# The last steps of the reciprocal root at the norms between blocks: on VectorE, in line with their use, and not on GpSimd

## What is computed

```python
def rmsnorm(x, g):
    xf = x.astype(jnp.float32)
    y = xf * lax.rsqrt(jnp.mean(xf * xf, axis=-1, keepdims=True) + EPS)
    return (y * g.astype(jnp.float32)).astype(x.dtype)

def second_block(x, ...):
    for i in range(DEPTH_2):
        h = rmsnorm(x, norm_mixer_pre[i])
        ...                                  # m = attention or convolution of h
        x = x + rmsnorm(m, norm_mixer_post[i])
        h = rmsnorm(x, norm_mlp_pre[i])
        x = x + rmsnorm(sq_relu_mlp(h, mlp_w_up[i], mlp_w_down[i]), norm_mlp_post[i])
    return x
```

## Time and profile before

| | us |
|---|---|
| Median of 3 runs | 2257.68 (2257.19 to 2259.3) |
| Profiled execution, its own time | 2260.75 |
| Its span, first to last instruction | 2259.0 |

### The profile page before, as it was taken

The page is one execution under the profiler, slowest core; times in us unless marked ns, Lnnn a source line. Parts: engine busy times, 40 slices in busy tenths (PEclk is TensorE's granted clock), DMA queues, the critical chain, the costliest instruction groups (busy, mean ns, idle before and its releaser), DMA issues.

```text
span 2259.0 us, 23194 instructions
## 1 busy us (share of the span) xinstructions
PE 2103.7 (93%) x9629; PEld 1740.1 (77%) x9629; DVE 1047.4 (46%) x930; ACT 751.8 (33%) x923; POOL 153.9 (7%) x311
## 2 busy tenths in 40 slices
PE   6998989989999999899887989999979977999997
PEld 5777778878888888688665778888868866888886
DVE  3345567654443243547544353333352355433434
ACT  3344463343323132422354342322341224322322
POOL 1000132000100000300000120000030003000001
PEclk9999999999999999899765989999989998999999
DMA  5211112123333222233100222332213222222331
GB/s 178 80 56 56 56 56 75 58 93 103 94 97 107 94 93 93 80 109 89 70 0 1 75 75 95 104 100 93 93 56 106 99 82 77 94 93 93 99 105 56
DMA packets 91339, 188.24 MB, mean 83 GB/s; under 512 B 3598, under 2 KB 3616, under 8 KB 91136
## 3 DMA queue, kind: packets, MB, share of 16 engines
q1 hardware_dynamic: 87744, 176.17, 23.6%
q0 software_dynamic: 3232, 10.21, 1.5%
q10 hardware_dynamic: 288, 0.79, 0.1%
HBM read 184.01 MB, written 2.10 MB: 82 GB/s over the span
## 4 chain that ended last, share of the span: by engine, by line
PE 81%; DVE 8%; ACT 4%; issue 3%; POOL 3%; DMA 1%; SPq 0%; POOLq 0%; ACTq 0%; DVEq 0%
PE ps L664 55%; PE ps L788 8%; PE ps L676 5%; PE ps L689 4%; PE ps L983 2%; PE ps L1012 1%; PE ps L892 1%; DVE w_lo L1456 1%; ACT w_hi L1058 1%; POOL small L516 1%; PE ps L714 1%; ACT qk L1123 1%; POOL small L518 1%; PE ps L816 1%; PE ps L843 1%
## 5 line engine op out<-in xcount | busy, mean ns | idle before, releaser
L1456 DVE TENSOR_TENSOR w_lo<-w_raw,w_hi 128x2048 fp32r<-128x2048 f32 x140 | 320.8, 2292 | 834.3 <-ACT w_hi L1058 834.3
L1058 ACT ACTIVATE w_hi<-w_raw 128x2048 fp32r<-128x2048 f32 x140 | 268.2, 1916 | 995.3 <-PE ps L664 877.3
L664 PE MATMUL ps<-a_hi,w_hi 128*128 128x512 f32 x1104 | 429.5, 389 | 0.0
L664 PE MATMUL ps<-a_lo,w_hi 128*128 128x512 f32 x1104 | 429.5, 389 | 0.0
L664 PE MATMUL ps<-a_hi,w_lo 128*128 128x512 f32 x1104 | 429.5, 389 | 0.0
L664 PE MATMUL ps<-w_hi,h_hi 128*128 128x512 f32 x672 | 262.9, 391 | 12.9 <-DVE h_lo L1500 9.3
L664 PE MATMUL ps<-w_lo,h_hi 128*128 128x512 f32 x672 | 262.5, 391 | 0.0
L664 PE MATMUL ps<-w_hi,h_lo 128*128 128x512 f32 x672 | 262.4, 390 | 0.0
L664 PEld LDWEIGHTS ps<-a_hi,w_hi 128*128 128x128 f32 x1104 | 207.2, 188 | 43.2
L664 PEld LDWEIGHTS ps<-a_lo,w_hi 128*128 128x128 f32 x1104 | 207.2, 188 | 42.8
L664 PEld LDWEIGHTS ps<-a_hi,w_lo 128*128 128x128 f32 x1104 | 207.2, 188 | 42.8
(11 more groups left out here) (299 smaller groups left out, 3153.9 us busy)
## 6 DMA issues: line engine op xcount, KB each, us to landing
w_raw<-in_w_ff SPq DMA_DIRECT2D x32, 1024.0 KB, 5.3
w_raw<-in_mlp_w_up SPq DMA_DIRECT2D x32, 1024.0 KB, 5.5
w_raw<-in_mlp_w_down SPq DMA_DIRECT2D x32, 1024.0 KB, 5.0
w_raw<-in_w_in SPq DMA_DIRECT2D x26, 1024.0 KB, 5.0
w_raw<-in_attn_w_qkv SPq DMA_DIRECT2D x12, 1024.0 KB, 5.3
w_raw<-in_conv_w_in SPq DMA_DIRECT2D x12, 1024.0 KB, 5.1
w_raw<-in_w_proj_gla SPq DMA_DIRECT2D x4, 1024.0 KB, 5.1
w_raw<-in_w_out SPq DMA_DIRECT2D x4, 1024.0 KB, 5.0
```

Of the source, the lines that this page charges most:

```text
L664: last = mm(ps[:, bank0 + j], left, right, start=(k == 0 and x == 0), stop=(k == QUAD * quads - 1 and x == 2), skip_group_check=halves)
L1058: nc.scalar.activation(w_hi[:, s], w_raw[:, s], ACT.Copy).then_inc(hi_ready, 1)
L1456: tt(w_lo[:, s], w_raw[:, s], w_hi[:, s].bitcast(F32), ALU.subtract).then_inc(lo_ready, 1)
```

## The change

The five instructions of a refinement leave GpSimd's queue and are issued by DVE, with the same operands, ahead of the instruction that multiplies the tile. DVE no longer waits for `rstd_ready`; it waits for ACT's sum ahead of the first of the five and for ACT's guess ahead of the second. Each of the five is followed by a wait of DVE for its own completion (`step`). GpSimd keeps its transfers. Nothing else is changed.

```diff
         @block.gpsimd
...
-            def refine(name, n, i):
-
-                pool.wait_ge(sumsq_ready, stat_count(name, n, i))
-                v, y, t, r, ss = (z[n % 2][:, i:i + 1] for z in (var, guess0, newton, rstd, sumsq))
-                pstep(nc.gpsimd.tensor_scalar(v, ss, 1.0 / D, EPS, ALU.mult, ALU.add))
-                pool.wait_ge(guess_ready, stat_count(name, n, i))
-                pstep(nc.gpsimd.tensor_tensor(t, y, y, ALU.mult))
-                pstep(nc.gpsimd.tensor_tensor(t, t, v, ALU.mult))
-                pstep(nc.gpsimd.tensor_scalar(t, t, -0.5, 1.5, ALU.mult, ALU.add))
-                nc.gpsimd.tensor_tensor(r, t, y, ALU.mult).then_inc(rstd_ready, 1)
...
             gain_row(g_turn, "norm_mlp", 0)
-            refine_tiles("h_mlp0")
             pool.wait_ge(normed, 8)
...
+            def tile_rstd(name, n, i):
+
+                dve.wait_ge(sumsq_ready, stat_count(name, n, i))
+                v, y, t, r, ss = (z[n % 2][:, i:i + 1] for z in (var, guess0, newton, rstd, sumsq))
+                step(ts(v, ss, 1.0 / D, EPS, ALU.mult, ALU.add))
+                dve.wait_ge(guess_ready, stat_count(name, n, i))
+                step(tt(t, y, y, ALU.mult))
+                step(tt(t, t, v, ALU.mult))
+                step(ts(t, t, -0.5, 1.5, ALU.mult, ALU.add))
+                step(tt(r, t, y, ALU.mult))
+
             def junction(name, move, rows, last_split, early_split=None):
...
                     if add is not None and 1 <= s_ <= TT:
                         i = s_ - 1
-                        dve.wait_ge(rstd_ready, stat_count(name, add, i))
+                        tile_rstd(name, add, i)
                         r = rstd[add % 2][:, i:i + 1]
...
                     if turn_ is not None and 2 <= s_ <= TT + 1:
                         i = s_ - 2
-                        dve.wait_ge(rstd_ready, stat_count(name, turn_, i))
+                        tile_rstd(name, turn_, i)
                         stt(y_tm[:, i], x_tm[:, i], rstd[turn_ % 2][:, i:i + 1], g_turn, ALU.mult, ALU.mult).then_inc(normed, 1)
```

More of the change, by code:

```diff
@@ L505, in _ @@
             dma = pool.dma_start
-            pstep = Steps(pool, pool_step)
             def gain_row(dst, name, row=None):
@@ L542, in _ @@
             assert r == N_GAINS
-            refine_tiles("h")
             pool.wait_ge(turned, turn_base["h"] + 8)
@@ L587, in _ @@
             gain_row(g_turn, "norm_mixer_pre_2", 0)
-            refine_tiles("h_mix1")
             pool.wait_ge(resid_ready, 4)
@@ L603, in _ @@
             gain_row(g_turn, "norm_mlp_pre_2", 0)
-            refine_tiles("h_mlp1")
             pool.wait_ge(normed, 16)
@@ L607, in _ @@
             gain_row(g_turn, "norm_mixer_pre_2", 1)
-            refine_tiles("h_conv")
             pool.wait_ge(chunk_lo, 4 + 2 * 16 + 8)
@@ L611, in _ @@
             gain_row(g_turn, "norm_mlp_pre_2", 1)
-            refine_tiles("h_mlp2")
             pool.wait_ge(normed, 24)
             gain_row(g_add, "norm_mlp_post_2", 1)
-            refine_tiles("out")
         @block.tensor
```

## The result

The changed kernel takes 2267.07 us (median of 8 runs, 2265.47 to 2269.05), the kernel before in the same session 2258.36 (8 runs): a ratio of 1.0037, 95% interval 1.0028 to 1.0045. A second session gave 2265.35 for 2259.38, 1.0026 (1.0015 to 1.0036). One run of the kernel before, in the session of e9 to e11, took 4185.09 us and is left out of the ratios there. The change costs 6 to 9 us. The forecast, 2268.5, lies within 1.5 us of the first median and 3.2 of the second, but as a difference it said 10.8 us, more than either interval holds.

A forecast was written before the change was run, and what follows sets the result against it. PE was taken to bound the kernel, DVE only at seven places; delays of 4.95 + 1.90 + 0.95 + 0.40 + 1.80 = 10.0 us plus 0.8 for the clock, on 2257.68, gave 2268.5 us, range 2264.2 to 2272.7.

The forecast's parts named there:

- What bounds the kernel, and which row decides: PE paces the kernel; DVE's staircase matters at seven places, decided by L1586 of tile 2, in `out` the last L1581.
- The price of a refinement on DVE: Five small DVE instructions 0.19 us apart cost 0.95 us per refinement, 0.76 after the guess where DVE comes early.
- The walk: DVE's staircase followed row by row through the junctions: decisive L1586 of `h_conv` 1.62 us later, `out` 1.80 later.
- The start: Junction `h`: tiles 1 and 2 do not hide their refinements, 1.90 us later, plus 0.8 us for TensorE's clock.
- The 0.8 for the clock: In `h`, longer PE idle time ahead of each tile brings a lower granted clock at restart, costing 0.8 us.
- Later decisive row is later product: In `h_mlp1`, `h_conv`, `h_mlp2` PE's restart follows the later L1586: 3 x 1.65 = 4.95 us.
- by a few tenths of a us, either way: At places other than `h`, where the clock is already down, a later restart shifts its rise only this much.
- The shared port: Rival: the five instructions vanish into gaps left by stretched GpSimd instructions; at a 0.10 step -3.6 us, 2254.1; chance 0.04.
- Absorbed: Rival: PE's restart hangs on something other than L1586 of tile 2; about 2.5 us remain, 2260.2; chance 0.09.
- The clock takes more: Rival: longer PE pauses bring the low clock into `h_mlp0` and `h_mix1` too; 14.5 us, 2272.2; chance 0.08.
- outside the junctions no stretch changed: Sign: the stretches between junctions keep their length, everything else being paced by PE and shifting with it.
- Its other signs: 220 small DVE instructions, 33 us more busy time; PE's transposes wait about 80 us; GpSimd's busy time less than half.

The follow-up runs named there:

- e9: Kernel before with the refinement in three instructions on GpSimd everywhere but in `h_mix1`, which keeps five: 2254.11 us for 2258.91, ratio 0.9974.
- e11: The kernel before itself, unchanged, one profiled execution for a second profile; its stretch from `h_mix1` to `h_mlp1` took 324.62 us.
- e5: Changed kernel with one more small instruction in each of the 44 refinements, six in place of five: 2276.37 us for 2259.14, ratio 1.0076.
- second pair: Second profile of the changed kernel (e12) against the second of before (e11); the shifts kept sum to 8.5 us.
- e12: The changed kernel again, unchanged, for a second profile and more times: 2265.35 us for 2259.38, ratio 1.0026.
- e1: Kernel before with the refinement moved to VectorE only in the first junction, `h`: 2260.27 us for 2258.50, ratio 1.0007.
- e2: Kernel before with the refinement moved to VectorE only in `h_mlp1`, `h_conv` and `h_mlp2`: 2261.79 us for 2258.50, ratio 1.0013.
- first pair: First profile of the changed kernel against the first of before; the shifts kept sum to 7.7 us.
- e10: Kernel before with the refinement in three instructions on GpSimd in `h_mix1` alone: 2260.09 us, ratio 1.0007.
- e6: Changed kernel with the refinement on VectorE in three instructions in place of five: 2263.85 us, ratio 1.0020.

## Why the prediction was right, and where it was not

- **What bounds the kernel, and which row decides.** Right: the loss comes from the places named, each decided by the row named. Nothing outside them took new instructions, but two stretches without one changed their length, see below.
- **The price of a refinement on DVE.** Right: 0.95 us at 0.19 per step. e5's sixth instruction moved the decisive row by 6 x 0.19 = 1.14 us, as the forecast counts six refinements ahead of it in line. The Trainium skill (VectorE: DVE Perf Modes, "The TRN2 errata") gives the duration of an fp32 tensor_tensor as (N + 151) cycles at 0.96 GHz; the estimate from it for one element, 0.158 us, agrees with the means of 0.146 to 0.160 us measured.
- **The walk.** Right: decisive rows 1.69 (1.62), 0.97 (0.95), 0.43 (0.36), 1.82 (1.80) us later.
- **The start.** `h`: the third turn instruction 1.91 us late in the second pair (forecast 1.9), and 2.1 us kept in the mean of the profiles, forecast 1.9 + 0.8. The 0.8 for the clock can be seen at PE's restart. The restart and the row at which the matmuls turn from 0.41 to 0.28 us, before and in the changed kernel:

```profile
24.64 0.56 PE L689 MATMUL ps<-a_hi,w_hi 128*128 128x256 f32 x1
25.22 0.31 PE L689 MATMUL ps<-a_hi,w_lo 128*128 128x256 f32 x1
...
27.07 0.56 PE L662 MATMUL ps<-a_hi,w_hi 128*128 128x256 f32 x1
31.28 0.38 PE L662 MATMUL ps<-a_lo,w_hi 128*128 128x256 f32 x1
```

They stand 0.21 us apart ahead of that row and 0.12 behind it. So the product of the kernel before, too, began at the lower clock, for 0.6 us (1.2 in e11), and not at the full one as the forecast read from the 1.00 of the earlier trace rows; that column shows 1.00 for the changed kernel from 25 to 31 us as well, where the matmuls stand 0.21 apart. The slow part is 4.2 us there, 2.9 in e12 and 2.5 in e1. From the third turn instruction to the first `w_lo` it takes 11.41, 10.78 and 10.61 us in these three, 9.74 and 10.09 in the two profiles of before; the restart itself stands 2.95 us behind that instruction in all five. So the clock took 0.5 to 1.7 us. Behind that, in a stretch that varies by 3.4 us between profiles with the same `h`, part of it is lost from sight.
- **"Later decisive row is later product", for the three junctions.** This term was mis-sized: 4.95 us in the sum, 3.2 kept in e2 and 3.2 in the second pair, 5.1 in the first pair. Likewise 0.40 for `h_mix1`, of which -0.26 to +0.26 was kept, and 0.95 for `h_mlp0`, of which 0.6 to 1.4 was. The step that failed is the sentence that at these places a later restart moves the clock's rise "by a few tenths of a us, either way". It is up to 1.4 us, and it does not average out here: without `h`, the decisive rows are 8.2 to 8.3 us late in both pairs, and 7.7 and 6.6 are kept; in e2 it is 5.1 and 3.2.
- **What makes up the difference.** `h_conv` shows both signs. At its restart the product runs longer at the lower clock, and 2.0 to 2.5 us are kept where 1.69 went in. Behind it, at the start of the last product ahead of `h_mlp2`, 1.1 to 1.4 come back. The kernel before, PE's timeline:

```profile
1842.04 0.77 PE L664 MATMUL ps<-w_hi,h_hi 128*128 128x512 f32 x1 [8.59 <-DVE h_lo L1500]
...
1847.72 0.52 PE L664 MATMUL ps<-w_lo,h_hi 128*128 128x512 f32 x1
```

and the changed one:

```profile
1847.07 0.77 PE L637 MATMUL ps<-w_hi,h_hi 128*128 128x512 f32 x1 [7.18 <-DVE h_lo L1473]
...
1850.62 0.48 PE L637 MATMUL ps<-w_hi,h_lo 128*128 128x512 f32 x1
```

The row of 0.52 and that of 0.48 us are where matmuls turn from 0.63 us (lower clock) to 0.39 (upper). It took 5.68 us from the restart in before and 3.55 us in the changed kernel. Of the 2.1 us in which before still ran slow, 1.0 us is lost time, and that is the 1.06 given back.
- **The rivals.** The shared port: GpSimd's instructions were indeed held by DVE's, and taking them away did win 0.3 us ahead of the first L1565, but the step of 0.19 decides, as worked out. Absorbed: wrong as put, since every decisive row moved. The clock takes more: wrong in the sign of its sum. It was the right mechanism with only one of its two directions, and so was the forecast's sign "outside the junctions no stretch changed": the stretch behind `h_conv` took 1.1 to 1.4 us less.
- **Its other signs.** 220 small instructions, 0.19 us apart, 32 us more busy time (33 forecast), 78.8 us for the wait of PE's transposes (80), GpSimd at 44% of its busy time, no wait of DVE for it: right. From the second L1616 of `h_conv` to the decisive L1586 it had 1.45 us; 1.69 came, and its own walk gives 1.62, since nothing ahead of that L1616 moves: a slip of the text, not of the sum.
- **The level.** The base was the other thing that helped: the medians of before are 2258.4 to 2259.4 in these sessions, 0.7 to 1.7 above the 2257.68 on which 10.8 was added. A sum too large by 2 us and a base too low by 0.7 gave a time off by 1.4. That it came so near is in part luck: the second session's 5.9 us lie below the 7.0 to 14.5 that the forecast had for its sum.

The version of e9 shows what the profile of before offered. The idle time of DVE was GpSimd's chain behind the guess. Two instructions in place of four shorten it (0.71 us from the start of L519 to the end of L520, before 1.01), and the large instructions beside it still hide the rest. GpSimd's timeline in e9's `h_conv`:

```profile
1656.50 0.34 POOL L519 TENSOR_SCALAR small<-small 128x1 f32<-128x1 f32 x1 [0.46 <-ACT small L1132]
1656.94 0.27 POOL L520 TENSOR_SCALAR small<-small 128x1 f32<-128x1 f32 x1
1657.45 1.13 POOL L517 TENSOR_SCALAR small<-small 128x1 f32<-128x1 f32 x1 [0.24 <-ACT qk L1129]
1658.67 1.32 POOL L519 TENSOR_SCALAR small<-small 128x1 f32<-128x1 f32 x1
```

and DVE's:

```profile
1657.24 1.28 DVE L1587 SCALAR_TENSOR_TENSOR y_tm<-y_tm,small,qk 128x1024 f32<-128x1024 f32 x1 [1.36 <-POOL small L520]
1658.56 1.23 DVE L1588 TENSOR_TENSOR x_tm<-x_tm,y_tm 128x1024 f32<-128x1024 f32 x1
1659.70 0.68 DVE L1622 TENSOR_TENSOR y_tm<-ps,y_tm 128x512 f32<-128x512 f32 x1
1660.40 1.28 DVE L1587 SCALAR_TENSOR_TENSOR y_tm<-y_tm,small,qk 128x1024 f32<-128x1024 f32 x1
```

The second L517 and L519 on GpSimd are again held until DVE's L1587 and L1588 end (1.13 and 1.32 us), and it costs nothing: the L1587 at 1660.40 has no idle time ahead of it. The decisive row is 1.86 us earlier than before in each of the three junctions, and 2.2, 1.2 and 0.65 us are kept.

**What stays open.** What sets the moment at which the clock rises was not tried; these runs show only when it did. How a difference inside `h_mix1` reaches the clock 170 us later, over work that runs the same to 0.03 us, is not shown either. Whether e9's gain of 0.26% would outlive another shift of `h_mix1` by some edit elsewhere is open too, since that one stretch alone is worth 4.3 us.

## What to carry to other kernels

A small step handed from one engine to another costs only the part that the receiver waits for; moved onto the busy engine it costs all of it, each time. Count the whole instruction distance (here 5 x 0.19 us) against the idle time that the waits show, tile by tile, and first make the chain behind the late input shorter where it is. When a change shifts a restart of TensorE, compare the unchanged stretches behind it as well: read both traces from junction to junction, and do not book a shift at a restart as a shift of the end.

## What the runs showed of the hardware that was not expected

- The granted clock of TensorE decides over as much as a good part of the change: the same matmuls at 1137 to 1148 us were granted 1.00 (e9) or 0.50 (e10) after a shift of 0.74 us in their start, 4.3 us in the length of the stretch, over 170 us behind the junction that was edited, with the work between the same to 0.03 us.
- At one place, the last product ahead of `h_mlp2`, the lower clock held for 5.68 us of work after a pause of 8.59 us (before), for 3.55 after 7.18 (the changed kernel) and for 2.7 after 5.9 (e2, e5, e12). It is no rule of the pause alone: in e6 it held for 5.69 us after 6.12.
- The column of the granted clock can be blind at the very start of a profile: it says 1.00 where the matmuls stand at the distance of the lower clock (27.07 to 31.28 us in the changed kernel).
- Small instructions are not all alike: on one column DVE's with three column operands takes 0.22 us against 0.15 to 0.16 for the others, and GpSimd's with two column scalars 0.34 against 0.18 for the one with two constants (e9's L517, undisturbed). A sum by count of instructions has to look at the form.
